# Eight of the 22 weight slots of the first feed-forward's up product computed as 2x2 block products

## The chip, the core and the metric

The kernel runs on one core of one Trainium2 chip. The metric is device time in microseconds (us) of one execution; of the kernel before, three runs are shown. A profiled execution gives the rows quoted below; its times count from its first instruction. Engines: PE is TensorE, DVE is VectorE, ACT is ScalarE, POOL is GpSimd, SP is SyncE, which here only issues weight transfers.

## What is computed

Two transformer blocks over 512 tokens of width 1024 in float32. The part that matters is the first block's feed-forward, whose up product `h @ w_up` has 5632 columns, followed by a causal convolution of width 3 along the tokens, a gelu on one half and a product with the other half:

```python
D_MODEL = 1024; SEQ = 512; D_FF = 2816; CONV_WIDTH = 3
h = _rmsnorm(x, g_pre_ffn[i])
u = _causal_dwconv(h @ w_up[i], w_conv[i], b_conv[i])
a, v = u[..., :D_FF], u[..., D_FF:]
x = x + _rmsnorm((jax.nn.gelu(a) * v) @ w_down[i], g_post_ffn[i])
```

The second block has two further feed-forwards (`up0`/`down0`, `up1`/`down1`) of width 4096 with a squared relu.

## The kernel before, in words

**Split products.** Every float32 product is made of three fp32r matmuls: both operands are split into a high part (ACT copies to fp32r) and a low part (DVE subtracts the high part from the original), and high x high, high x low and low x high are summed in PSUM. So each weight block costs ACT one "high" copy (`L1074`) and DVE one "low" subtraction (`L1745`) before PE may use it; semaphores `w_hi` and `w_lo` count them.

**Weight ring.** SP loads weights in slots of 1 MB (two transfers of 512 KB) into `raw`, which has two places. Slot n may be loaded when both ends of slot n-2 have been split. The split halves go to `WHL`, a ring of six half places of 128x512. A unit of 128x1024 takes two half places, a block of 128x512 takes one. `upto(w)` says which units may be split once unit w has been used by PE.

**The up stage.** `w_up` has 22 slots (j = 0 to 21). Slot j holds 128 columns of the a half and the 128 columns of the v half that belong to them: two units, s = 0 and 1. For each unit PE makes one group: 8 steps of k x 3 matmuls with 512 token columns, into one of banks 0 to 3 (`feature_product`, lines 2609 to 2611). The first four groups are made in two token halves by `norm_halves`. When a group is done, ACT scales it by the last tap into `cv` (`L1488`), DVE adds the other two taps, reading the bank again (`L2213`, two instructions), ACT takes the gelu of the a half (`L1496`) and DVE multiplies (`L2224`) into `uT`. Each engine works through a written-out order, so an instruction that waits holds up all behind it on its engine. ACT and DVE split a weight unit after each unit of the convolution.

**The block product of the second block's feed-forwards.** In `up0` and `up1` the last 12 slots are computed otherwise. The slot's 1024x256 weights are read as 2x2 blocks A11, A12, A21, A22 (512x128 each), the activations as B11, B12, B21, B22 (512x256 each), and seven products replace eight. POOL makes four sums of weight blocks per slot (S1, S2, S4, S3, lines 864 to 869), DVE makes four sums of activation blocks once per feed-forward, PE makes seven products of 12 matmuls with 256 columns (lines 3321 to 3323), ACT copies the first result (`st_m1`), and DVE adds the results with seven 128x256 additions (`L2410`). S1 and S2 lie in `GB`, S4 in `PB`, S3 over A11's place in `raw`.

Of the kernel before, what the change touches and what calls it, by code (L numbers as in the profile page):

```python
# [26 lines left out]
F32 = mybir.dt.float32  # L27
# [53 lines left out]
NSUM = 7  # L81

# [29 lines left out]
def weight_slots(t):  # L112
# [86 lines left out]
    for name in ("kq0",) + DENSE_KV:  # L199
# [3 lines left out]
        else:  # L203
# [12 lines left out]
          ("merge", 16, "act"), ("br", 16, "vec"), ("up", 2 * NFF, "conv"),  # L216
# [3 lines left out]
          ("dv1", 4, "vec"), ("kq3", 4, "act"), ("up1", NCL, "act")]  # L220

# [62 lines left out]
def strassen_slot(name, i):  # L284

    return name in UPS and 2 * i >= NCL
# [6 lines left out]
def program(nc, t, out):  # L293
    with ExitStack() as ctx:
# [68 lines left out]
        cv = PB[:, 0:3072].rearrange("p (b a t) -> p b a t", b=2, a=3)  # L363
# [166 lines left out]
        lhs_sum, rhs_sum, rhs_hi, rhs_lo = (sem(s) for s in ("lhs_sum", "rhs_sum", "rhs_hi", "rhs_lo"))  # L530
        st_full, st_keep, st_sum, sq_ready = (sem(s) for s in (
# [25 lines left out]
        for n, (name, i, _) in enumerate(slots):  # L557
            if strassen_slot(name, i):
                for j, part in enumerate(LHS):
                    unit_at[name, part, i - NCL // 2] = len(units)  # L560
# [36 lines left out]
        for n, (name, i, _) in enumerate(slots):  # L597
            g0 = GT[name][0] if name in GT else None
            if strassen_slot(name, i):
                for j in range(len(LHS)):  # L600
                    unit_free.append((st_full, len(LHS) * (NPAIR * int(name[2:]) + i - NCL // 2) + j + 1))
                slot_free.append((w_lo, len(unit_free)))
            elif name not in WHOLE:
                for j in range(2):
# [189 lines left out]
        def _(pool):  # L794
# [58 lines left out]
            def block_sums(l, gain):  # L853

                n, name = 4 + 2 * l, UPS[l]

                def lhs_sums(q):

                    i = slot_at[name, NCL // 2 + q]
                    at = len(SUMS) * (NPAIR * l + q)  # L860
# [11 lines left out]
                for q in range(NPAIR):  # L872
                    lhs_sums(q)
                if gain is not None:
                    pool.wait_ge(w_lo, unit_at[name, "S1", NPAIR - 1] + 1)
                    pool.dma_start(GB[:, :], gain.to_broadcast([P, D])).then_inc(gain_in, 16)

            def resid(r):
# [33 lines left out]
                if r in (3, 5):  # L912
                    block_sums((r - 3) // 2, nxt[r + 1])
# [92 lines left out]
            pool.wait_ge(x_ready, 4)  # L1006
            pool.dma_start(ptok, t["p"][0, 0].rearrange("(t p) c -> p t c", p=P)).then_inc(p_in, 16)
# [59 lines left out]
        def _(act):  # L1067
# [10 lines left out]
            def split(w):  # L1078

                while done[0] <= min(w, n_units - 1):  # L1080
# [5 lines left out]
                    elif strassen_slot(*slots[units[u][0]][:2]) and LHS[units[u][1]][0] == "S":  # L1086
                        name, i = slots[units[u][0]][:2]
                        q = NPAIR * int(name[2:]) + i - NCL // 2
# [388 lines left out]

            for j in range(NFF):
                if j == 10:
                    for k in range(2):  # L1480
                        act.wait_ge(pt_in_psum, k + 1)
                        copy(pTh[:, k, :], bank[4 + k][:, :]).then_inc(pt_hi, 1)
                if j >= 2:
                    act.wait_ge(u_ready, j - 1)
                for s in range(2):
                    f = s * NFF + j
                    wait_group("up", 2 * j + s)
                    a.activation(cv[:, j % 2, s, :], bank[(GT["up"][0] + 2 * j + s) % 4][:, :], ACT.Identity,  # L1488
                                 bias=cols[:, C_BCONV + f:C_BCONV + f + 1],
                                 scale=tapcol(2, f)).then_inc(conv_act, 1)  # L1490
                    if f < 2 * NFF - 1:
                        split(unit_at["up", 2 * j + s] + HL)
                    if j == NFF - 1 and s == 0:
                        rows_begin(uT, "down", lambda k: (u_ready, k + 1))
                act.wait_ge(conv_vec, 2 * j + 1)
# [59 lines left out]
            def mlp(name, l):  # L1555
# [24 lines left out]
                for c in range(NCL):  # L1580
                    plain(c)
                    if c in (1, 2, 3, 4):
                        rhs_high(c - 1)
                    if c >= 2:
                        split(upto(unit_at[name, c]))
                for q in range(NPAIR):
                    n = NPAIR * l + q
                    split(upto(unit_at[name, "A11", q]))
                    act.wait_ge(st_full, len(LHS) * n + 2)
                    if n:  # L1590
                        act.wait_ge(st_sum, NSUM * (n - 1) + 2)
                    copy(st_m1, st_bank(q, 0)).then_inc(st_keep, 1)
# [127 lines left out]
        def _(vec):  # L1720
# [477 lines left out]

            for j in range(NFF):
                if j == 10:  # L2200
                    for k in range(2):
                        vec.wait_ge(pt_hi, k + 1)
                        v.tensor_tensor(pTl[:, k, :], bank[4 + k][:, :], pTh[:, k, :].bitcast(F32),
                                        ALU.subtract).then_inc(pt_lo, 1)
                for s in range(2):
# [3 lines left out]
                    b = wait_group("up", 2 * j + s)  # L2209
                    vec.wait_ge(conv_act, 2 * j + s + 1)  # L2210
                    y = cv[:, j % 2, s, :]
                    for tap, sh in ((1, 1), (0, 2)):
# [5 lines left out]
                        else:  # L2218
                            ins.then_inc(conv_vec, 1)
                    if f < 2 * NFF - 1:  # L2220
                        split(unit_at["up", 2 * j + s] + HL)
                vec.wait_ge(conv_vec, 2 * j + 2)
# [1323 lines left out]
```

## Time and profile before

| What | Value |
|---|---|
| Median of 3 runs | 2040.4 us (2039.64 to 2042.12) |
| Profiled execution, its own time | 2039.82 us |
| Its span, first to last instruction | 2038.1 us |
| PE busy | 2017.6 us, 99% of the span |
| DVE, ACT, POOL busy | 1227.8, 928.0, 411.6 us |
| Up stage on PE, groups 5 to 44 | 427.3 to 645.8 us |
| Granted TensorE clock | 0.999 of full speed |

The time of the execution is 1.7 us above its span. A row of the timeline gives start, duration, engine, line, operation, what it writes and reads, and how many in a row; durations of neighbours overlap by about 0.1 us, so the distance between two starts, called the pitch below, says what an instruction costs its engine.

### The profile page before, as it was taken

Reading aid. Unit: us, or ns where it says so; the run is one execution under the profiler, and the core shown is the slowest. Engines: PE = TensorE matmul, PEld = TensorE weight load, DVE = VectorE, ACT = ScalarE, POOL = GpSimd, SP = SyncE. Lnnn points to the kernel's source line nnn. Section 1 sums busy time; section 2 is a strip of 40 time slices with the busy share of each in tenths; the row PEclk is TensorE's granted clock in tenths of the full one; section 3 lists DMA queues with packets and bytes.
Section 4 is the critical chain, followed back from the end, with each engine's and each line's share of the span. In section 5 each row is a group of like instructions: output and inputs, shape, how many; then the busy total and the mean of one; then the engine's idle time right before and its main releaser. Section 6 shows DMA issues by size and latency. Waiting matters only on the chain.

```text
span 2038.1 us, 31753 instructions
## 1 busy us (share of the span) xinstructions
PE 2017.6 (99%) x12798; PEld 1695.7 (83%) x12798; DVE 1227.8 (60%) x2042; ACT 928.0 (46%) x1708; POOL 411.6 (20%) x402
## 2 busy tenths in 40 slices
PE   8999999999999999999999999999999999999998
PEld 7987567888888888878888999888877779999887
DVE  4744766565555344676676899433655558897334
ACT  4345664443333334523335566322545556665322
POOL 7500000000000000223331365000533112562000
PEclk9999999999999999999999999999999999999999
DMA  7336412333333222222213233332332232233222
GB/s 170 102 96 91 58 42 93 94 104 103 95 92 104 103 104 93 79 83 80 84 43 104 80 100 109 118 104 96 121 94 83 73 101 66 84 104 135 104 85 81
DMA packets 167535, 191.18 MB, mean 94 GB/s; under 512 B 18818, under 2 KB 137133, under 8 KB 167389
## 3 DMA queue, kind: packets, MB, share of 16 engines
q1 hardware_dynamic: 163469, 175.25, 27.3%
q0 software_dynamic: 3904, 13.90, 3.7%
q8 instruction: 101, 1.65, 0.3%
q14 instruction: 45, 0.37, 0.1%
q10 hardware_dynamic: 16, 0.00, 0.0%
HBM read 181.79 MB, written 7.34 MB: 93 GB/s over the span
## 4 chain that ended last, share of the span: by engine, by line
PE 96%; DVE 2%; ACT 1%; issue 0%; POOL 0%; DMA 0%; POOLq 0%; DVEq 0%; ACTq 0%
PE bank L2710 27%; PE bank L2609 9%; PE bank L2610 8%; PE bank L2611 8%; PE bank L3323 4%; PE bank L3322 4%; PE bank L3321 4%; PE bank L2648 2%; PE bank L2650 2%; PE bank L2649 2%; PE bank L3224 2%; PE bank L2881 1%; PE bank L3226 1%; PE bank L3225 1%; PE bank L3245 1%; PE bank L3247 1%
## 5 line engine op out<-in xcount | busy, mean ns | idle before, releaser
L1745 DVE TENSOR_TENSOR WHL<-raw,WHL 128x1024 fp32r<-128x1024 f32 (+2 forms) x357 | 458.7, 1292 | 441.9 <-ACT WHL L1074 441.6
L1074 ACT ACTIVATE WHL<-raw 128x1024 fp32r<-128x1024 f32 (+2 forms) x357 | 334.1, 939 | 511.3 <-PE bank L2710 325.3
L2710 PE MATMUL bank<-WHL,HXh 128*128 128x512 f32 x1344 | 362.3, 390 | 0.0
L2609 PE MATMUL bank<-HXh,WHL 128*128 128x512 f32 x752 | 298.3, 397 | 0.0
L2710 PEld LDWEIGHTS bank<-WHL,HXh 128*128 128x128 f32 x1344 | 251.3, 188 | 52.8 <-issue 1.2
L2611 PE MATMUL bank<-HXh,WHL 128*128 128x512 f32 x752 | 293.2, 390 | 0.0
L2610 PE MATMUL bank<-HXl,WHL 128*128 128x512 f32 x576 | 224.3, 389 | 0.0
L2710 PE MATMUL bank<-WHL,HXl 128*128 128x512 f32 x672 | 208.4, 389 | 0.0
L2609 PEld LDWEIGHTS bank<-HXh,WHL 128*128 128x128 f32 x752 | 141.1, 188 | 33.3 <-issue 3.7
L2611 PEld LDWEIGHTS bank<-HXh,WHL 128*128 128x128 f32 x752 | 141.1, 188 | 30.3
L888 POOL TENSOR_SCALAR small<-small 128x1 f32<-128x1 f32 x24 | 7.8, 324 | 761.0 <-ACT PB L1162 760.9
L2710 PEld LDWEIGHTS bank<-WHL,HXl 128*128 128x128 f32 x672 | 126.1, 188 | 26.2
L2213 DVE SCALAR_TENSOR_TENSOR PB<-bank,cols,PB 128x511 f32<-128x511 f32 x88 | 66.0, 750 | 101.6 <-ACT PB L1488 100.0
L2610 PEld LDWEIGHTS bank<-HXl,WHL 128*128 128x128 f32 x576 | 108.3, 188 | 21.1
L1488 ACT ACTIVATE PB<-bank,cols 128x512 f32<-128x512 f32 x44 | 34.4, 781 | 141.8 <-PE bank L2611 136.0
L830 POOL TENSOR_TENSOR raw<-raw,cols 128x1024 f32<-128x1024 f32 x24 | 46.0, 1932 | 221.7 <-DMA raw<-in_b_w_q_dram 211.2
L3323 PE MATMUL bank<-HXh,WHL 128*128 128x256 f32 x288 | 81.5, 283 | 0.0
L3322 PE MATMUL bank<-HXl,WHL 128*128 128x256 f32 x288 | 81.5, 283 | 0.0
L3321 PE MATMUL bank<-HXh,WHL 128*128 128x256 f32 x288 | 81.5, 283 | 0.0
L2610 PE MATMUL bank<-HX2l,WHL 128*128 128x512 f32 x176 | 68.6, 390 | 0.0
L1025 POOL TENSOR_TENSOR PB<-BIG,PB 128x512 f32<-128x512 f32 x24 | 39.6, 1650 | 142.3 <-PE bank L3188 101.3
L864 POOL TENSOR_TENSOR GB<-raw 128x512 f32<-128x512 f32 x24 | 38.8, 1616 | 138.4 <-DVE WHL L1745 91.3
(380 smaller groups left out, 4440.8 us busy)
## 6 DMA issues: line engine op xcount, KB each, us to landing
raw<-in_mlp_w_up_dram SPq DMA_DIRECT2D x64, 512.0 KB, 4.7
raw<-in_mlp_w_down_dram SPq DMA_DIRECT2D x64, 512.0 KB, 4.1
raw<-in_w_up_dram SPq DMA_DIRECT2D x44, 512.0 KB, 5.1
raw<-in_a_w_in_dram SPq DMA_DIRECT2D x32, 512.0 KB, 4.6
raw<-in_w_in_dram SPq DMA_DIRECT2D x22, 512.0 KB, 4.8
raw<-in_w_down_dram SPq DMA_DIRECT2D x22, 512.0 KB, 3.7
raw<-in_w_kv_dram SPq DMA_DIRECT2D x16, 512.0 KB, 4.5
rel_dram<-GB POOLq DMA_DIRECT2D x1, 5120.0 KB, 54.5
```

Source lines behind the costliest of these rows:

```text
L830: g.tensor_tensor(w, w, cols[:, c:c + nk].unsqueeze(2).to_broadcast([P, nk, D // nk]), ALU.mult).then_inc(w_scaled, 1)
L1074: return a.activation(dst, src, ACT.Copy, **k)
L1745: v.tensor_tensor(dst(1), src, dst(0).bitcast(F32), ALU.subtract).then_inc(w_lo, 1)
L2213: ins = v.scalar_tensor_tensor(out=y[:, sh:T], in0=b[:, 0:T - sh], scalar=tapcol(tap, f), in1=y[:, sh:T], op0=ALU.mult, op1=ALU.add)
L2609: m.matmul(b[:, :], w[0][:, k, :], x[0][:, k, :], start=(k == 0), stop=False)
L2610: m.matmul(b[:, :], w[0][:, k, :], x[1][:, k, :], start=False, stop=False)
L2611: return m.matmul(b[:, :], w[1][:, k, :], x[0][:, k, :], start=False, stop=(k == KD - 1))
L2648: m.matmul(b[:, sl], wh[:, k, :], HXh[:, k, sl], start=(k == 0), stop=False)
L2710: ins = m.matmul(ybank(tt, h, 1 if name == "down" else 0)[:, :], x, w[:, h * HALF:(h + 1) * HALF], start=(k == 0 and i == 0), stop=(k == n ...
L3321: m.matmul(dst, wh[:, k, :], x[0][:, k, :], start=(k == 0), stop=False)
L3322: m.matmul(dst, wh[:, k, :], x[1][:, k, :], start=False, stop=False)
L3323: ins = m.matmul(dst, wl[:, k, :], x[0][:, k, :], start=False, stop=(k == KD // 2 - 1))
```

## The change

Slots j = 6, 8, 10, ..., 20 of the up stage (`UPJ`) become block products; the odd slots and the first six stay as they were. For such a slot:

- PE makes 84 matmuls with 256 columns instead of 48 with 512, into banks 4 to 7. Before each block slot but the first it waits until all seven additions of the last one are done.
- ACT and DVE split seven blocks of 128x512 instead of two units of 128x1024.
- POOL makes four 128x512 sums; ACT copies one 128x256 result; DVE makes seven additions. The sums land in `uT`, and the convolution then reads `uT` (SBUF) instead of the bank.
- DVE makes the activation sums in slots 0 to 3 (nine 128x1024 instructions), ACT their high parts in slots 1 to 4, DVE their low parts in slots 4 and 5.
- A slot of blocks takes seven of the ring's half places; the eighth is skipped and counted as used by the last block.

`cv` moves from `PB` to `BIG`, S4 to `BIG`, the transposes of the other input from slot 10 to slot 9, its load ahead of POOL's block sums, and the load of `g_post_ffn` behind them. The code for `up0` and `up1` becomes shared functions with the same order of work.

```diff
+PTURN = 9
+UPJ = (6, 8, 10, 12, 14, 16, 18, 20)
...
-    return name in UPS and 2 * i >= NCL
+    return name in UPS and 2 * i >= NCL or name == "up" and i in UPJ
...
-                ring_before[w] = latest.get(ring_place[w] + n - 1)
+                ring_before[w] = max((latest[ring_place[w] + h] for h in range(n) if ring_place[w] + h in latest),
+                                     default=None)
                 for h in range(n):
                     latest[ring_place[w] + h] = w
                 half_place += n
+                if slots[units[w][0]][0] == "up" and n == 1 and units[w][1] == len(LHS) - 1:
+                    latest[half_place % (2 * HL)] = w
+                    half_place += 1
...
+            def pair_begin(name, q):
+
+                n = PAIR0[name] + q
+                split(upto(unit_at[name, "A11", q]))
+                act.wait_ge(st_full, len(LHS) * n + 2)
+                if n:
+                    act.wait_ge(st_sum, NSUM * (n - 1) + 2)
+                copy(partial(name)[0], st_bank(name, q, 0)).then_inc(st_keep, 1)
+
             for j in range(NFF):
...
                 if j >= 2:
                     act.wait_ge(u_ready, j - 1)
+                if j in (1, 2, 3, 4):
+                    rhs_high(0, j - 1)
+                if j in UPJ:
+                    q = UPJ.index(j)
+                    pair_begin("up", q)
+                    for part in LHS[1:]:
+                        split(upto(unit_at["up", part, q]))
...
+            def pair_sums(name, q, row1, row2, early=None, late=None):
...
+                vec.wait_ge(st_full, at + 2)
+                vec.wait_ge(st_keep, n + 1)
+                add(c11, m1, 1)
+                split(upto(unit_at[name, "A11", q]))
+                split(upto(unit_at[name, "A12", q]))
+                vec.wait_ge(st_full, at + 4)
+                add(u2, m1, 3)
+                split(upto(unit_at[name, "S4", q]))
+                split(upto(unit_at[name, "S2", q]))
...
             for j in range(NFF):
...
+                if j in (4, 5):
+                    for i in (0, 1) if j == 4 else (2, 3):
+                        rhs_low(0, i)
+                if j in UPJ:
+                    q = UPJ.index(j)
+                    pair_sums("up", q, uT[:, j, :], uT[:, j + 1, :])
                 for s in range(2):
                     f = s * NFF + j
...
-                    b = wait_group("up", 2 * j + s)
+                    b = uT[:, j + s, :] if j in UPJ else wait_group("up", conv_tile(j, s))
...
+                    if j in UPJ:
+                        if s:
+                            split(upto(unit_at["up", "A22", q]))
+                    elif f < 2 * NFF - 1:
+                        split(upto(unit_at["up", 2 * j + s]))
...
+                if j < 4:
+                    rhs_block(0, j, 1)
...
+            for j in range(2, NFF):
+                if j in UPJ:
+                    q = UPJ.index(j)
+                    if q:
+                        pe.wait_ge(st_sum, NSUM * q)
+                    if j > PTURN:
+                        pe.wait_ge(pt_lo, 2)
+                    block_pair("up", q)
+                    continue
```

**How it stands on DVE, slots 12 and 13.** Before, two slots are twice this piece (two taps from a bank, one weight unit, again, the product; line numbers are of before):

```order
L2213 SCALAR_TENSOR_TENSOR PB<-bank0,cols,PB 128x511 [waits conv_act,ps_full]
L2213 SCALAR_TENSOR_TENSOR PB<-bank0,cols,PB 128x510 [waits vec_chain]
L1745 TENSOR_TENSOR WHL<-raw,WHL 128x1024 [waits w_hi]
L2213 SCALAR_TENSOR_TENSOR PB<-bank1,cols,PB 128x511 [waits conv_act,ps_full]
L2213 SCALAR_TENSOR_TENSOR PB<-bank1,cols,PB 128x510 [waits vec_chain]
L1745 TENSOR_TENSOR WHL<-raw,WHL 128x1024 [waits w_hi]
L2224 TENSOR_TENSOR BIG<-PB 128x512 [waits gelu_ready,conv_vec]
```

In the changed kernel the block slot begins with the additions (`L2286`); the last block, A22, is split behind the first of them, and then come the taps from SBUF, the next block slot's first two blocks, and the product (line numbers are of the changed kernel, `L1791` is the split):

```order
L2286 TENSOR_TENSOR BIG<-PB,bank4 128x256 [waits st_keep,st_full]
L1791 TENSOR_TENSOR WHL<-raw,WHL 128x512 [waits w_hi]
L2286 TENSOR_TENSOR BIG<-PB,bank5 128x256 [waits st_full]
L1791 TENSOR_TENSOR WHL<-raw,WHL 128x1024 [waits w_hi]
L2286 TENSOR_TENSOR BIG<-BIG,bank6 128x256 [waits st_sum,st_full]
...
L1791 TENSOR_TENSOR WHL<-raw,WHL 128x1024 [waits w_hi]
L2330 SCALAR_TENSOR_TENSOR BIG<-BIG,cols 128x511 [waits conv_act]
L2330 SCALAR_TENSOR_TENSOR BIG<-BIG,cols 128x510 [waits vec_chain]
L2330 SCALAR_TENSOR_TENSOR BIG<-BIG,cols 128x511 [waits conv_act]
L2330 SCALAR_TENSOR_TENSOR BIG<-BIG,cols 128x510 [waits vec_chain]
L1791 TENSOR_TENSOR WHL<-raw,WHL 128x512 [waits w_hi] x2
L2349 TENSOR_TENSOR BIG<-BIG 128x512 [waits gelu_ready,st_conv]
```

What moved: the next block slot's A11 and A12 now stand behind four tap instructions whose two large operands both lie in SBUF.

**How it stands on ACT, slot 1.** Before, the gelu of slot 0 (`L1496`) is followed at once by the first convolution instruction of slot 1; after (`L1550` is the gelu, `L1102` the copies) one copy stands between them that waits for the activation sum `rhs_sum`. Before:

```order
L1496 ACTIVATE PB<-PB 128x512 [waits conv_vec]
L1488 ACTIVATE PB<-bank2,cols 128x512 [waits ps_full]
```

and after:

```order
L1550 ACTIVATE BIG<-BIG 128x512 [waits conv_vec]
L1102 ACTIVATE HX2l<-PB 128x1024 [waits rhs_sum]
```

What moved: the convolution of slot 1 and the weight copy behind it now come after DVE's first activation sum, which on DVE is three 128x1024 instructions behind the product of slot 0.

## Rows read from the trace of the kernel before

**Rows 1.** The page, busy time and share of the span of each engine.
```profile
PE 2017.6 (99%) x12798; PEld 1695.7 (83%) x12798; DVE 1227.8 (60%) x2042; ACT 928.0 (46%) x1708; POOL 411.6 (20%) x402
```

**Rows 2.** Waits, 420 to 650 us: who waited for whom, total, times, longest.
```profile
ACT PB L1488 <- PE bank L2611: 136.0, 40, 3.7
DVE PB L2213 <- ACT PB L1488: 100.0, 44, 2.7
```

**Rows 3.** Line 2611 in 424 to 646 us: count, durations in ns, first and last start.
```profile
L2611 PE MATMUL bank<-HXh,WHL x320: 389/389/393, 427.7 to 645.6; 128*128 128x512 f32 x160
```

**Rows 4.** Timeline of PE: transposes in the up stage; first block matmul, end of `up0`.
```profile
514.35 1.03 PE L3090 MATMUL bank<-ident,BIG 128*128 128x128 f32 x8
515.14 0.48 PE L2609 MATMUL bank<-HXh,WHL 128*128 128x512 f32 x1
...
1152.68 0.28 PE L3321 MATMUL bank<-HXh,WHL 128*128 128x256 f32 x1
...
1273.63 1.55 PE L2710 MATMUL bank<-WHL,HX2l 128*128 128x512 f32 x6
```

**Rows 5.** Timeline of ACT and DVE in the up stage, one unit.
```profile
503.66 0.78 ACT L1488 ACTIVATE PB<-bank,cols 128x512 f32<-128x512 f32 x1 [3.65 <-PE bank L2611]
504.34 1.05 ACT L1074 ACTIVATE WHL<-raw 128x1024 fp32r<-128x1024 f32 x1
...
504.55 1.53 DVE L2213 SCALAR_TENSOR_TENSOR PB<-bank,cols,PB 128x511 f32<-128x511 f32 x2 [2.71 <-ACT PB L1488]
506.00 1.22 DVE L1745 TENSOR_TENSOR WHL<-raw,WHL 128x1024 fp32r<-128x1024 f32 x1
507.13 0.69 DVE L2224 TENSOR_TENSOR BIG<-PB 128x512 f32<-128x512 f32 x1
```

**Rows 6.** Timeline of DVE and POOL in `up0`, one block slot.
```profile
1176.82 3.16 DVE L1745 TENSOR_TENSOR WHL<-raw,WHL 128x512 fp32r<-128x512 f32 x2
1179.91 0.41 DVE L2410 TENSOR_TENSOR PB<-PB,bank 128x256 f32<-128x256 f32 x1
1180.24 1.45 DVE L1745 TENSOR_TENSOR WHL<-raw,WHL 128x512 fp32r<-128x512 f32 x1
...
1183.64 1.07 DVE L2410 TENSOR_TENSOR BIG<-PB,bank 128x256 f32<-128x256 f32 x3
1184.64 0.68 DVE L1745 TENSOR_TENSOR WHL<-GB,WHL 128x512 fp32r<-128x512 f32 x1
1185.24 0.41 DVE L2410 TENSOR_TENSOR BIG<-BIG,bank 128x256 f32<-128x256 f32 x1
...
1177.81 1.63 POOL L866 TENSOR_TENSOR GB<-GB,raw 128x512 f32<-128x512 f32 x1
1179.51 1.62 POOL L868 TENSOR_TENSOR PB<-raw,GB 128x512 f32<-128x512 f32 x1
```

**Rows 7.** Timeline of POOL and DVE at the first block sums of `up0`.
```profile
1139.67 1.29 POOL L866 TENSOR_TENSOR GB<-GB,raw 128x512 f32<-128x512 f32 x1
1141.04 2.16 POOL L868 TENSOR_TENSOR PB<-raw,GB 128x512 f32<-128x512 f32 x1
...
1139.76 2.29 DVE L1745 TENSOR_TENSOR WHL<-raw,WHL 128x1024 fp32r<-128x1024 f32 x1 [1.32 <-ACT WHL L1074]
```

**Rows 8.** Slot loads: SP's issues of one slot; the page's time to landing.
```profile
447.46 0.99 SPq L778 DMA_DIRECT2D raw<-in_w_up_dram  x2
...
raw<-in_w_up_dram SPq DMA_DIRECT2D x44, 512.0 KB, 5.1
```

**Rows 9.** Timeline of ACT in `up0`, two high parts of blocks.
```profile
1171.42 1.14 ACT L1074 ACTIVATE WHL<-GB 128x512 fp32r<-128x512 f32 x2
```

**Rows 10.** Timeline of DVE, first activation sum of `up0`: three instructions from 1121.21.
```profile
1121.21 1.22 DVE L2383 TENSOR_TENSOR PB<-HXl 128x1024 f32<-128x1024 f32 x1
...
1124.85 1.22 DVE L2376 TENSOR_TENSOR PB<-HXh,PB 128x1024 f32<-128x1024 f32 x1
```

**Rows 11.** Timeline of DVE, product of slot 0 in the up stage.
```profile
424.54 0.69 DVE L2224 TENSOR_TENSOR BIG<-PB 128x512 f32<-128x512 f32 x1 [0.41 <-ACT PB L1496]
```

More of the change, by code:

```diff
@@ L2197, in _ @@
             border(0)
-            for j in range(NFF):
[L2200 to L2204, printed above, removed]
+            (b11, b11l), (b12, b12l), (b21, b21l), (b22, b22l) = (
+                [x.bitcast(F32) for x in rhs(part)] for part in ("B11", "B12", "B21", "B22"))
@@ L3085, in _, with block @@
             norm_halves(1)
[L3086 to L3092 removed]
+            def block(name, q, part, x, i):
+                w = unit_at[name, part, q]
+                pe.wait_ge(w_lo, w + 1)
+                wh, wl = (split_buf(w, j).rearrange("p (k c) -> p k c", k=KD // 2) for j in range(2))
+                dst = st_bank(name, q, i)
+                for k in range(KD // 2):
+                    m.matmul(dst, wh[:, k, :], x[0][:, k, :], start=(k == 0), stop=False)
+                    m.matmul(dst, wh[:, k, :], x[1][:, k, :], start=False, stop=False)
+                    ins = m.matmul(dst, wl[:, k, :], x[0][:, k, :], start=False, stop=(k == KD // 2 - 1))
+                ins.then_inc(st_full, 1)
@@ new lines, in block_pair @@
+            def block_pair(name, q):
+                o = 4 * SETS.index(name)
+                block(name, q, "A11", rhs("B11"), 0)
+                block(name, q, "A12", rhs("B21"), 1)
+                block(name, q, "S4", rhs("B22"), 2)
+                if q == 0:
+                    pe.wait_ge(rhs_lo, o + 2)
+                block(name, q, "S2", rhs_sums(1), 3)
+                block(name, q, "S1", rhs_sums(0), 4)
+                if q == 0:
+                    pe.wait_ge(rhs_lo, o + 3)
+                block(name, q, "S3", rhs_sums(2), 5)
+                if q == 0:
+                    pe.wait_ge(rhs_lo, o + 4)
+                block(name, q, "A22", rhs_sums(3), 6)
@@ new lines, in _ @@
+            for j in range(2, NFF):
+                if j in UPJ:
+                    q = UPJ.index(j)
[5 more added lines that the diff above has]
+                    continue
+                for s in range(2):
+                    if j == PTURN and s:
+                        pe.wait_ge(p_in, 16)
+                        pe.wait_ge(st_sum, NSUM * sum(1 for i in UPJ if i < j))
+                        for k in range(2):
+                            for tt in range(TT):
+                                ins = m.transpose(bank[4 + k][:, tt * P:(tt + 1) * P],
+                                                  ptok[:, tt, k * P:(k + 1) * P], ident[:, :])
+                            ins.then_inc(pt_in_psum, 1)
+                    w = [y.rearrange("p (k c) -> p k c", k=KD) for y in unit("up", 2 * j + s)]
+                    b = group("up", conv_tile(j, s))
+                    for k in range(KD):
+                        ins = feature_product(b, w, (HXh, HXl), k)
+                    ins.then_inc(ps_full, 1)
@@ L3308, in _, with block_pairs @@
                     out_product(k, (tt,))
[L3310 to L3324 removed]
+            def block_pairs(name):
                 for q in range(NPAIR):
```

267 lines of the change are left out of this document (128 added, 139 removed).

## The prediction

> **What bounds the kernel now.** I read the page first: PE is busy 99% of the span, DVE 60%, ACT 46% [rows 1]. Then the waits of the up stage, to see who sets its pace: ACT waits 136.0 us there for PE, once in each of 40 groups, DVE waits 100.0 us for ACT, and PE's feature products wait for nobody [rows 2]. So the up stage lasts as long as PE's matmuls, and each microsecond of PE work removed is gained, as long as DVE, ACT, POOL and the slot loads still keep ahead.
>
> **PE, removed.** One matmul with 512 columns costs the distance to the next. Line 2611 is every third of 960 matmuls: from the first to the last of its 320 starts there are 217.9 us and 957 steps [rows 3], with the transposes between (514.35 to 515.14, 0.8 us [rows 4]): 217.1/957 = 0.227 us. A plain slot has 48: 10.89 us. A matmul with 256 columns: the 12 block slots of `up0` take 1152.68 to 1273.63 for 1008 matmuls, 0.120 us each, with no stall [rows 4]. A block slot has 84: 10.08 us. Eight slots save 8 x 0.81 = **6.5 us**, 0.32%. That is all the change can give. About 0.2% (4.1 us) is what a measurement of this kernel can tell from no change.
>
> **DVE, added.** Pitches: two tap instructions from a bank 1.45 us, a 128x1024 low part 1.13 [rows 5]; a 128x256 addition 0.33, a 128x512 low part 0.60 [rows 6], the product likewise 0.60. Taps that read only SBUF stand in no row: not below 0.60 (the 128x512 instruction of two SBUF operands [rows 6]), not above 0.75 (the bank taps with their semaphore); I take 0.70, nearest the bank taps, since the same chain wait stays. A plain slot costs 2 x 1.45 + 2 x 1.13 + 0.60 = 5.8 us; a block slot 7 x 0.33 + 7 x 0.60 + 4 x 0.70 + 0.60 = 9.9. Together 15.7 of the 20.97 us that PE now has for two slots. That alone would fit.
>
> **What POOL does to DVE.** While POOL makes block sums, DVE's instructions on two SBUF operands come out longer: two 128x512 low parts take 3.09 us from start to start instead of 1.20, 0.94 us more each; a third takes 1.45 instead of 0.68. The addition between them reads a bank and keeps its 0.41 [rows 6]. With a larger neighbour: a low part issued at 1139.76, just behind POOL's 1139.67, ends at 1142.05, so with its own 1.22 it began at 1140.83, 1.16 after POOL; and POOL's next, issued at 1141.04, takes 2.16 because it now waits for DVE [rows 7]. So the two take turns, and POOL holds DVE for 0.94 to 1.16 us a time; I take 1.05. Four sums a slot give DVE up to 4.2 us more: 19.9 of 20.97. And the change puts the taps of block slots (BIG,cols and BIG) among the instructions that are held, which the bank taps are not.
>
> The Trainium skill (SBUF — State Buffer, "Who interferes with whom" and the reading of its diagram) states this as a lock: a VectorE instruction with two SBUF inputs and a GpSimd instruction that reads SBUF exclude each other for the whole instruction. If the whole recorded 1.62 us of a POOL sum were the hold, DVE would need 15.7 + 6.5 = 22.2 of 20.97 us and each pair of slots would be 1.2 us late; the rows of this case give 1.05, since 1.62 includes POOL's own wait for DVE.
>
> **The loop that decides.** Average load is not enough, because there is a ring of waits from one block slot's A22 to the next, with no PE in it:
> 1. A22's low part done, so SP loads the next block slot: the second issue about 0.5 us after the first, landed 5.1 later [rows 8], semaphore 0.1: 5.7.
> 2. ACT's high parts of A11 and A12 come ahead of its convolution instruction: 1.05 (1.14 less the overlap) [rows 9], then 0.89 from ACT's start to DVE's [rows 5]: 1.9.
> 3. Four taps, 2.8. POOL starts its sums with the same landing, so its second is running when the taps begin: held 0.4 + 1.05 + 1.05 = 2.5. Together 5.3.
> 4. Low parts A11, A12 (1.2), product (0.6), next plain slot's taps (1.45), S4 and S2 (1.2), taps (1.45), S1 and S3 (1.2), product (0.6), first addition (0.33), A22 (0.7): 8.7.
>
> Sum 21.6 us against 20.97 on PE: **0.65 us late per round**. Being late shows first at PE's A11 and S4: A11's low part is ready 5.7 + 1.9 + 5.3 + 0.6 + 0.2 = 13.7 after the last A22, so A22 may be 7.2 us into its slot at most; S4 follows A11 by 3.3 us where PE allows 2.9, so 6.9. At the first block slot the two late activation parts (2 x 1.13), the taps, four blocks, the product, an addition and A22 put A22 at about 6.5. That leaves 0.4 of slack; seven rounds cost 7 x 0.65 - 0.4 = 4.2 us.
>
> **The start.** DVE ends slot 0's product at 425.2 [rows 11]. The first activation sum is three instructions, 3.64 us to the next start [rows 10]: 428.8. Only then ACT makes its high part (0.95), the convolution of slot 1 (0.68) and the high part of the sixth unit (0.95): 431.4. DVE does its taps from 430.7 to 432.1, the low part to 433.3. PE's fifth group began at 427.3, two matmuls ahead of the first start in [rows 3], and ends 24 x 0.227 = 5.4 later, at 432.7: 0.6 us of stall. At slots 4 and 5, four low parts of 1.13 meet POOL's first sums, which hold DVE up to four times; the unit needed there would be ready about 0.3 late (between 0 and 2). Start: **1.0 us**.
>
> At no cost: ACT, whose added 2.1 us per two slots (7 x 0.53 + 0.3 less 2 x 0.95) lie in its 136 us of waiting [rows 2]; the moved transposes (same number); the moved `g_post_ffn` load, needed only behind `down`; PE's wait for all additions, which has a plain slot of 10.9 us between, and would cost only if DVE were that late.
>
> **Sum:** -6.5 + 1.0 + 4.2 = -1.3 us on the profiled execution's 2039.82: 2038.5. The median of the runs shown lies 0.6 above that execution: **2039.1**.
>
> **Rivals.**
> - *Full gain.* The loop is 0.65 too long by terms of which I am not sure: with 0.63 for an SBUF tap (-0.3), holds of 0.95 (-0.3) and a landing 0.2 earlier it is below 20.97 and only the start remains: -6.5 + 0.6 to 1.0, so 2034.5 to 2034.9. For it: DVE's sum of 19.9 fits. Against: the order of waits above. Up to a loop of 21.3 it is still faster by over 4.1.
> - *Slower.* The same loop, longer: holds of 1.16 (+0.3), taps of 0.75 (+0.2), a landing 0.3 later and another hold on the low parts A11, A12 (+1.05 every round if POOL's fourth sum reaches them). From 22.3 us on it decides: 7 x 1.4 - 0.4 + 1.0 - 6.5 = +3.9; with the whole lot 23.2, +10: 2050.
> - *A hold of 1.62 us each time,* POOL's recorded duration: the holds in step 3 grow by 3 x 0.57, loop 23.3, +12: 2052. The turns in [rows 6, 7] speak against it; I give it 0.02, inside the slower rival. (It is what the rule of the Trainium skill, SBUF — State Buffer, gives if the recorded span is taken for the instruction's own.)
> - *The start alone costs more:* 2 to 3 us, if the high part that ACT makes ahead of each slot's convolution delays slots 2 to 4 as well. There each sum is two instructions and PE allows more than 1 us. Then 2041, within the same case.
>
> **How the numbers follow.** Loop between 21.0 and 22.2, result -4.1 to +4: 0.58. Full or nearly full gain: 0.28. Slower by over 0.2%: 0.14. Faster, same and slower are these three. The range goes to 2034.5, the full gain, and to 2044, as the slow rival beyond it has about 1 in 10.
>
> **What the changed profile would show.** The block line in the up stage at 0.120 us a matmul, a block slot 10.1 us where nothing is late. PE waiting about 0.6 us in the sixth group and 0.3 to 1 us at A11 or S4 of the later block slots, ended by DVE's low part. DVE taps in block slots of 1.7 to 1.8 us where they meet POOL, 0.7 where not. DVE over 90% busy from slot 6 on. Period of two slots 21.3 to 21.8 us. The prediction is wrong if that period is 20.97 (loop short enough), or over 22.3; also if PE waits for the additions instead of the low parts, which I did not price.

## The result and the profile after

| | Before | Changed |
|---|---|---|
| Median | 2040.12 us (2039.64 to 2042.12, 6 runs) | 2048.34 us (2046.93 to 2049.06, 6 runs) |
| Span of the profiled execution | 2038.1 us | 2046.4 us |
| PE, first matmul of `down` | 645.79 us | 653.46 us |

The ratio is 1.0038, with a 95% interval from 1.0028 to 1.0049: the changed kernel is 8.2 us slower. The prediction was 2039.1 us with a range to 2044.0, so it was wrong, and on the wrong side of the range. Of the 8.3 us by which the span grew, 7.7 us have arisen by the end of the up stage; 0.6 us come behind it.

The page of the changed kernel, busy time by engine, and the share of the engines in the chain that ended last. In the page of before the chain was PE for 96%:

```profile
PE 2016.9 (99%) x13086; PEld 1706.6 (83%) x13086; DVE 1295.7 (63%) x2151; ACT 949.8 (46%) x1760; POOL 461.2 (23%) x434
...
PE 86%; DVE 7%; DMA 3%; ACT 2%; issue 2%; POOL 0%; SPq 0%; POOLq 0%; DVEq 0%; ACTq 0%
```

PE has hardly less busy time than in [rows 1], although 6.5 us of matmuls were to go; and 12% of the chain now run over DVE, DMAs and ACT, where it was 3% before. Both ask for PE's own rows. The timeline of PE in the changed kernel, those rows at which it had waited (`L2682` to `L2684` are the plain matmuls, `L3168` to `L3170` those of the blocks, `L2785` is `down`):

```profile
433.27 0.50 PE L2682 MATMUL bank<-HXh,WHL 128*128 128x512 f32 x1 [0.45 <-DVE WHL L1791]
...
514.43 0.39 PE L2684 MATMUL bank<-HXh,WHL 128*128 128x512 f32 x1
520.67 0.55 PE L3168 MATMUL bank<-HXh,WHL 128*128 128x256 f32 x1 [5.85 <-DVE pb_rest L2345]
...
586.61 0.36 PE L3168 MATMUL bank<-HXh,WHL 128*128 128x256 f32 x1 [0.25 <-DVE WHL L1791]
...
653.46 2.77 PE L2785 MATMUL bank<-WHL,HX2h 128*128 128x512 f32 x11 [1.79 <-DVE HX2h L1800]
```

The large one stands ahead of slot 10: 514.43 to 520.67 where 0.23 is the pitch, 6.0 us lost. Its releaser is not a weight block but `pb_rest`, the low parts of the transposes of the other input (`pe.wait_ge(pt_lo, 2)` for j > PTURN in the diff): the transposes lie in banks 4 and 5, which the block slot writes over, so they must have been split first. What follows the pause is in the windows of PE, DVE, ACT and POOL there; PEclk is the granted clock as a share of 2.4 GHz:

```profile
core 0: us, PE busy (x) PEld busy (x) DVE busy (x) ACT busy (x) POOL busy (x), PEclk, DMA share, GB/s
510.00:515.00 5.00, 4.82 (x22) 3.66 (x20) 4.93 (x5) 2.58 (x6) 3.51 (x3) 1.00 0.00 1
515.00:520.00 5.00, 0.00 (x0) 0.00 (x0) 4.96 (x9) 3.12 (x6) 0.00 (x0) 0.94 0.00 0
520.00:525.00 5.00, 4.33 (x20) 4.36 (x21) 3.78 (x6) 0.63 (x1) 0.00 (x0) 0.50 0.00 0
525.00:530.00 5.00, 5.00 (x40) 5.00 (x39) 1.44 (x3) 1.21 (x2) 0.00 (x0) 0.88 0.19 54
```

After the pause PE runs at the lower of its two levels, 1.2 GHz. Of the rows of the timeline of PE, two before and two behind the return of the clock show it in the pitch, 0.21 and 0.12 us:

```profile
525.50 0.41 PE L3169 MATMUL bank<-HXl,WHL 128*128 128x256 f32 x1
525.72 0.41 PE L3170 MATMUL bank<-HXh,WHL 128*128 128x256 f32 x1
...
526.41 0.28 PE L3168 MATMUL bank<-HXh,WHL 128*128 128x256 f32 x1
526.53 0.28 PE L3169 MATMUL bank<-HXl,WHL 128*128 128x256 f32 x1
```

Some 26 matmuls cost 0.21 instead of 0.12 us; block slot 10 lasts 12.57 us (520.67 to 533.24) instead of 10.07. That is a part of why PE's busy time hardly shrank, and not the larger one. From 427.2 us to `down` PE is busy for 218.6 us before and 217.3 here; e1_turn3 below, whose clock stays up, still has 216.5, and e6_all, which has no stalls, 212.1. A short stall shows only in part as idle time: the row behind it is longer (0.36 us at 586.61, where the rows beside it have 0.28) and overlaps the wait. The Trainium skill (TensorE: Matmul & The Clock Gate, "What's actually happening") says that the throttled state is the default and work releases the clock; the rows agree, 0.94 in the window without a matmul and 0.50 right behind it.

Where the 7.7 us come from, by the starts of PE's slots (plain slots otherwise 10.90, block slots 10.08):

| Term | Predicted | Measured |
|---|---|---|
| Matmuls removed | -6.5 | -6.5 |
| Start, up to slot 6 (first block matmul at 471.7) | +1.0 | +1.0 |
| Pause ahead of slot 10 | 0 | +6.1 |
| Lower clock in slot 10 | 0 | +2.5 |
| Stalls in all other slots from 6 to 20 | +4.2 | +2.5 |
| Slot 21, ahead of `down` | 0 | +2.0 |
| Sum | -1.3 | +7.6 |

The 6.1 us of the pause are slot 9's 17.81 us less the 10.90 of a plain slot and 0.8 for the transposes; the gap between the two rows gives 6.0.

Now the loop. ACT, POOL and DVE around the landing of slot 16, and PE at S4 of that slot, as the timelines have them (`L1102` high parts, `L1537` convolution, `L2330` taps, `L891` to `L896` POOL's sums, `L895` being S4):

```profile
577.08 0.99 SPq L804 DMA_DIRECT2D raw<-in_w_up_dram  x2
...
578.42 1.16 ACT L1102 ACTIVATE WHL<-raw 128x512 fp32r<-128x512 f32 x2 [3.24 <-DMA raw<-in_w_up_dram]
578.46 1.30 POOL L891 TENSOR_TENSOR GB<-raw 128x512 f32<-128x512 f32 x1 [15.71 <-DMA raw<-in_w_up_dram]
...
579.48 1.51 ACT L1537 ACTIVATE BIG<-BIG,cols 128x512 f32<-128x512 f32 x2
579.84 1.30 POOL L893 TENSOR_TENSOR GB<-GB,raw 128x512 f32<-128x512 f32 x1
...
580.31 5.55 DVE L2330 SCALAR_TENSOR_TENSOR BIG<-BIG,cols 128x511 f32<-128x511 f32 x4 [3.26 <-ACT BIG L1537]
...
581.22 1.61 POOL L895 TENSOR_TENSOR BIG<-raw,GB 128x512 f32<-128x512 f32 x1
...
582.80 1.73 POOL L896 TENSOR_TENSOR raw<-raw 128x512 f32<-128x512 f32 x1
...
585.78 1.29 DVE L1791 TENSOR_TENSOR WHL<-raw,WHL 128x512 fp32r<-128x512 f32 x2
...
589.03 0.68 DVE L1791 TENSOR_TENSOR WHL<-BIG,WHL 128x512 fp32r<-128x512 f32 x1
...
589.77 0.39 PE L3168 MATMUL bank<-HXh,WHL 128*128 128x256 f32 x1
```

One landing starts three engines. ACT makes two high parts first, from 578.42 to 579.48, and only then the convolution for which DVE waits, idle for 3.26 us; by then POOL is in its second sum, and DVE's four taps take 5.47 us (580.31 to 585.78). PE is 0.2 us late at S4 as well (589.77, 0.34 behind its last matmul of A12 where 0.12 is the pitch); POOL had made S4 at 582.83, and what came last was DVE's low part, at 589.71. The groups by form, 475 to 650 us (count, busy us, mean ns of one), show the two kinds of taps side by side:

```profile
L2330 DVE SCALAR_TENSOR_TENSOR BIG<-BIG,cols 128x511 f32<-128x511 f32 x16 | 23.5, 1471 | 24.3 <-ACT BIG L1537 24.3
L2330 DVE SCALAR_TENSOR_TENSOR BIG<-BIG,cols 128x510 f32<-128x510 f32 x16 | 18.4, 1149 | 0.6
L2330 DVE SCALAR_TENSOR_TENSOR BIG<-bank,cols,BIG 128x510 f32<-128x510 f32 x15 | 11.2, 749 | 0.5
L2330 DVE SCALAR_TENSOR_TENSOR BIG<-bank,cols,BIG 128x511 f32<-128x511 f32 x15 | 11.2, 744 | 0.0
```

With both large operands in SBUF a tap takes 1.47 or 1.15 us, from a bank 0.75.

### The profile page after: what moved, and what is told of

Its sections match the earlier page's. It is cut to its first block, busy times and chain, and to the rows that moved or that the text cites. A ratio compares the mean times of both kernels' runs of the same rounds, so it can differ in the third digit from the quotient of the medians.

```text
span 2046.4 us, 32576 instructions
## 1 busy us (share of the span) xinstructions
PE 2016.9 (99%) x13086; PEld 1706.6 (83%) x13086; DVE 1295.7 (63%) x2151; ACT 949.8 (46%) x1760; POOL 461.2 (23%) x434
## 4 chain that ended last, share of the span: by engine, by line
PE 86%; DVE 7%; DMA 3%; ACT 2%; issue 2%; POOL 0%; SPq 0%; POOLq 0%; DVEq 0%; ACTq 0%
PE bank L2785 27%; PE bank L2682 5%; PE bank L2684 5%; PE bank L2683 5%; PE bank L3168 4%; PE bank L3170 4%; PE bank L3169 4%; DVE BIG L2330 2%; DMA raw<-in_w_up_dram 2%; PE bank L2721 2%; PE bank L2723 2%; PE bank L2722 2%; DVE WHL L1791 2%; PE bank L3344 1%; PE bank L2956 1%
## 5 line engine op out<-in xcount | busy, mean ns | idle before, releaser
L1791 DVE TENSOR_TENSOR WHL<-raw,WHL 128x1024 fp32r<-128x1024 f32 (+2 forms) x373 | 461.4, 1245 | 442.6 <-ACT WHL L1102 442.3
L1102 ACT ACTIVATE WHL<-raw 128x1024 fp32r<-128x1024 f32 (+2 forms) x373 | 336.5, 907 | 577.5 <-PE bank L2785 328.3
L2785 PE MATMUL bank<-WHL,HXh 128*128 128x512 f32 x1344 | 362.3, 390 | 0.0
L2785 PEld LDWEIGHTS bank<-WHL,HXh 128*128 128x128 f32 x1344 | 251.4, 188 | 52.8 <-issue 1.2
L2682 PE MATMUL bank<-HXh,WHL 128*128 128x512 f32 x624 | 248.9, 399 | 0.5 <-DVE WHL L1791 0.5
L2684 PE MATMUL bank<-HXh,WHL 128*128 128x512 f32 x624 | 243.4, 390 | 0.0
L2785 PE MATMUL bank<-WHL,HXl 128*128 128x512 f32 x672 | 208.4, 389 | 0.0
L2683 PE MATMUL bank<-HXl,WHL 128*128 128x512 f32 x448 | 174.7, 390 | 0.0
L2785 PEld LDWEIGHTS bank<-WHL,HXl 128*128 128x128 f32 x672 | 126.1, 188 | 26.2
L2682 PEld LDWEIGHTS bank<-HXh,WHL 128*128 128x128 f32 x624 | 117.2, 188 | 29.2 <-issue 4.0
L2684 PEld LDWEIGHTS bank<-HXh,WHL 128*128 128x128 f32 x624 | 117.2, 188 | 25.3
L891 POOL TENSOR_TENSOR GB<-raw 128x512 f32<-128x512 f32 x32 | 50.0, 1562 | 304.0 <-DMA raw<-in_w_up_dram 165.7
L3168 PE MATMUL bank<-HXh,WHL 128*128 128x256 f32 x384 | 110.6, 288 | 6.8 <-DVE pb_rest L2345 5.9
L3169 PE MATMUL bank<-HXl,WHL 128*128 128x256 f32 x384 | 109.7, 286 | 0.0
L3170 PE MATMUL bank<-HXh,WHL 128*128 128x256 f32 x384 | 109.7, 286 | 0.0
L2683 PEld LDWEIGHTS bank<-HXl,WHL 128*128 128x128 f32 x448 | 84.3, 188 | 15.9
L3168 PEld LDWEIGHTS bank<-HXh,WHL 128*128 128x128 f32 x384 | 74.8, 195 | 9.2 <-issue 8.2
L3169 PEld LDWEIGHTS bank<-HXl,WHL 128*128 128x128 f32 x384 | 74.9, 195 | 0.2
L3170 PEld LDWEIGHTS bank<-HXh,WHL 128*128 128x128 f32 x384 | 74.8, 195 | 0.0
L3168 PE MATMUL bank<-HX2l,WHL 128*128 128x256 f32 x256 | 72.4, 283 | 0.0
```

The source lines that it names most:

```text
L891: g.tensor_tensor(lhs(i, "S1"), lhs(i, "A21"), lhs(i, "A22"), ALU.add).then_inc(lhs_sum, 1)
L1102: return a.activation(dst, src, ACT.Copy, **k)
L1791: v.tensor_tensor(dst(1), src, dst(0).bitcast(F32), ALU.subtract).then_inc(w_lo, 1)
L2682: m.matmul(b[:, :], w[0][:, k, :], x[0][:, k, :], start=(k == 0), stop=False)
L2683: m.matmul(b[:, :], w[0][:, k, :], x[1][:, k, :], start=False, stop=False)
L2684: return m.matmul(b[:, :], w[1][:, k, :], x[0][:, k, :], start=False, stop=(k == KD - 1))
```

## The experiments

The theory after reading the trace: POOL's hold makes DVE late (the loop); at slot 10 the same lateness meets the wait for the transposes' low parts, and the clock drops behind it. The rivals: that the transposes' new place alone does the damage (then the kernel with them elsewhere shows the full gain); that the SBUF taps are slow by themselves. "D" is how the first matmul of `down` stands to 645.79 of before.

| Kernel | Median (range), us | Ratio to before, 95% | D, us |
|---|---|---|---|
| e1_turn3 | 2045.05 (2044.22 to 2046.04) | 1.0024 [1.0015, 1.0033] | +4.5 |
| e2_turn3_tiny | 2034.98 (2034.17 to 2035.43) | 0.9975 [0.9965, 0.9985] | -5.6 |
| e10_tiny9 | 2034.81 (2034.57 to 2035.27) | 0.9974 [0.9964, 0.9984] | -5.5 |
| e3_actfirst | 2038.97 (2037.12 to 2039.31) | 0.9993 [0.9984, 1.0002] | -0.9 |
| e4_four | 2037.74 (2037.58 to 2038.90) | 0.9989 [0.9980, 0.9998] | -2.3 |
| e5_both | 2035.91 (2035.68 to 2036.53) | 0.9980 [0.9971, 0.9989] | -4.2 |
| e7_late | 2036.93 (2035.56 to 2038.21) | 0.9985 [0.9976, 0.9994] | -2.2 |
| e9_ptfirst | 2035.52 (2034.87 to 2036.24) | 0.9977 [0.9969, 0.9986] | -4.7 |
| e6_all | 2033.81 (2033.71 to 2033.99) | 0.9970 [0.9958, 0.9981] | -6.5 |

The kernel before had a median of 2039.8 to 2040.0 us beside them.

**The transposes moved to slot 3.**

```diff
-PTURN = 9
+PTURN = 3
```

> The changed kernel with one number changed: the eight transposes of the other input stand in slot 3 instead of slot 9, long before the first block slot, so no block slot waits for their low parts on DVE. Theory A (two separate losses: 6.1 us of waiting for these low parts plus 2.4 us of matmuls at the lower TensorE clock behind it; and a loop of waits DVE - slot load - ACT - taps - DVE of 21.8 us against 20.97 on PE): the 8.5 us go, but the 6.1 us pause had also given the loop slack, and without it seven rounds late by 0.8 us come back, with 2 us at the start of down: -6.5 + 1.0 + 5.2 + 2 = +1.7 us against the kernel before, about 2042. Theory B (the transposes alone throw DVE late; the loop is a consequence): nearly the full gain, -5.5 us, about 2034.6.

Measured: 2045.05. The pause and the clock's drop are gone, but only 3.3 us came back. The period from one block slot to the next is now 21.5, 22.1, 22.3, 22.0, 21.7, 21.9 and 21.7 us, 6.4 us in all over 7 x 20.98, and slot 21 lasts 12.71 us. So the loop is too long from the first round on. In the changed kernel it cost only 2.5 us because the pause and the slow slot behind it, 8.6 us together, had given DVE time to catch up: the first whole round in its wake is at 20.98, the next three at 21.5, 21.8 and 21.7. The rival of the place alone is out. PE's waiting row ahead of slot 10 is now of the size and kind predicted for the loop:

```profile
517.49 0.36 PE L3168 MATMUL bank<-HXh,WHL 128*128 128x256 f32 x1 [0.59 <-DVE WHL L1791]
```

The start is 2.4 us late here: DVE makes the transposes' low parts at 453.42 (1.2 us), and the activation sums' low parts behind them come under POOL's first sums for longer (4.57 instead of 3.46 us for two). The 2042 expected was missed by 3 us: the start cost 2.4 and not 1.0, the rounds 6.4 and not 5.2.

**The same, with POOL's sums of this feed-forward cut to 8 of 512 elements.** The weight sums are thereby left out of the computation; DVE, ACT and PE do all their instructions.

```diff
+def part_of_block(i, part):
+    return lhs(i, part)[:, 0:1, 0:8] if name == "up" else lhs(i, part)
...
-g.tensor_tensor(lhs(i, "S1"), lhs(i, "A21"), lhs(i, "A22"), ALU.add).then_inc(lhs_sum, 1)
+g.tensor_tensor(part_of_block(i, "S1"), part_of_block(i, "A21"), part_of_block(i, "A22"), ALU.add).then_inc(lhs_sum, 1)
```

and so for S2, S4 and S3.

> As the run with the transposes in slot 3, and POOL's four block sums of each block slot of the first feed-forward are cut to 8 elements per partition (that part of the weight sums is left out; the order, the waits and all other work stay). Theory A with POOL's hold as its decisive term: the taps take 2.8 to 3.0 us instead of 5.5 and the loop falls to about 19.2 us, below 20.97: no stall at block slots, only the start's 1.0 us, -5.5 us, about 2034.6. If DVE is late by its own added work and not by POOL, the time is that of the run with full sums.

Measured: 2034.98. Every block slot lasts 10.08, every plain slot 10.90 us, with no stall after the start. The groups by form of DVE, 475 to 640 us:

```profile
L2334 DVE SCALAR_TENSOR_TENSOR BIG<-BIG,cols 128x510 f32<-128x510 f32 x16 | 12.0, 751 | 0.6
L2334 DVE SCALAR_TENSOR_TENSOR BIG<-BIG,cols 128x511 f32<-128x511 f32 x16 | 12.0, 748 | 11.1 <-ACT BIG L1541 11.1
```

The SBUF taps take the 0.75 us of a bank tap. They are not slow; POOL held them. This kernel takes both POOL's hold and the time of the sums away and cannot by itself tell one from the other; but where PE waited for S4 in the rows above, POOL had made it 6.9 us before DVE's low part was done.

**The same cut (the weight sums left out), with the transposes in slot 9** as in the changed kernel.

```diff
-PTURN = 3
+PTURN = 9
```

> The changed kernel with the transposes left in slot 9, and POOL's block sums of the first feed-forward cut to 8 elements on one of the four sub-blocks (so the weight sums are left out of the computation). The slots before showed a pause of 5.85 us ahead of the block slot after the transposes. If that pause is only DVE's being late, and DVE is late only because POOL holds it, the pause goes together with the loop: block slot 10 at 10.1 us, clock 1.0, and a time within 1 us of the same cut with the transposes in slot 3 (2035.0), so 2034.5 to 2035.5. If the place of the transposes costs a wait of its own (their low parts stand behind taps and a weight split on DVE, whoever held it), a pause of 2 to 6 us stays in slot 9 and the time is 2037 to 2043.

Measured: 2034.81. The timelines of DVE and PE:

```profile
505.55 2.98 DVE L2334 SCALAR_TENSOR_TENSOR BIG<-BIG,cols 128x511 f32<-128x511 f32 x4 [1.35 <-ACT BIG L1541]
...
512.90 1.28 DVE L2349 TENSOR_TENSOR pb_rest<-bank,pb_rest 128x512 fp32r<-128x512 f32 x2
...
514.01 0.39 PE L2688 MATMUL bank<-HXh,WHL 128*128 128x512 f32 x1
514.28 0.36 PE L3172 MATMUL bank<-HXh,WHL 128*128 128x256 f32 x1
```

against these of the changed kernel:

```profile
500.31 5.38 SPq L804 DMA_DIRECT2D raw<-in_w_up_dram  x4
...
507.47 1.15 ACT L1102 ACTIVATE WHL<-raw 128x512 fp32r<-128x512 f32 x2 [4.73 <-DMA raw<-in_w_up_dram]
...
509.37 5.55 DVE L2330 SCALAR_TENSOR_TENSOR BIG<-BIG,cols 128x511 f32<-128x511 f32 x4 [4.75 <-ACT BIG L1537]
514.83 1.29 DVE L1791 TENSOR_TENSOR WHL<-raw,WHL 128x512 fp32r<-128x512 f32 x2
...
519.29 1.28 DVE L2345 TENSOR_TENSOR pb_rest<-bank,pb_rest 128x512 fp32r<-128x512 f32 x2
```

The pause goes with the hold: one root for both losses. With DVE free the low parts end at about 514.2, and PE goes on at 514.28, 0.05 us late: the wait has no slack at all, and whatever DVE is late there, PE is late in full. In the changed kernel the taps start 3.8 us later (509.37 against 505.55) and take 2.6 us more; the low parts start 6.4 us later. Of the 3.8 us, 2.6 are the slot load's issue (500.31 against 497.74, because DVE's low part of A22 was late by as much after the held taps of the round before), and 1.3 its landing (7.2 us from issue to ACT's start against 5.9).

**ACT's order.** In a block slot ACT makes its two convolution instructions, and only then the high parts of A11 and A12 that wait for the slot load.

```diff
-                    for part in LHS[1:]:
+                    for part in LHS[1:-1]:
                         split(upto(unit_at["up", part, q]))
...
+                if j in UPJ:
+                    split(upto(unit_at["up", "A22", q]))
                 act.wait_ge(*((st_conv, 2 * q + 1) if j in UPJ else (conv_vec, conv_tile(j) + 1)))
```

> The changed kernel with one thing moved on ACT: in a block slot its two convolution instructions stand ahead of the high parts of the next block slot's A11 and A12, which wait for the slot's load. The transposes stay in slot 9. Theory A: DVE's taps begin about 3 us earlier, before POOL's sums, and leave the loop, which falls to about 18 to 19 us; the waiting for the transposes' low parts shrinks from 6.1 to 1 to 3 us, and the clock stays up if the pause is short; the 2 us at the start of down go. -6.5 + 1.0 + 1 to 3 = -4.5 to -2.5 us, about 2036.6. Theory B: the wait in slot 10 stays as it is, 2045 or above.

Measured: 2038.97. The work is the same, and from slot 12 on every round is at 20.98 us. The timeline of ACT and DVE in slot 14:

```profile
571.29 1.52 ACT L1537 ACTIVATE BIG<-BIG,cols 128x512 f32<-128x512 f32 x2 [0.33 <-DVE BIG L2288]
573.28 1.15 ACT L1102 ACTIVATE WHL<-raw 128x512 fp32r<-128x512 f32 x2 [0.48 <-DMA raw<-in_w_up_dram]
...
572.75 5.85 DVE L2332 SCALAR_TENSOR_TENSOR BIG<-BIG,cols 128x511 f32<-128x511 f32 x4
```

The convolution no longer waits for the landing, so the taps start before it and are off the loop; they are held just as much (1.44 and 1.13 us each). But the pause ahead of slot 10 is still 2.8 us, and the matmuls behind it run at the lower clock. This kernel missed the 2036.6 us expected of it by 2.4 us for that reason: taking the convolution off the loop does not shorten the queue ahead of the transposes' low parts enough. The slow matmuls seem not to come in every execution: of its eleven, eight have a span of 2037.0 to 2037.2 us, as the profiled one, and three have 2035.3, 2035.3 and 2036.0. The difference is about the 1.5 us of the clock, but these three left no trace, so this is not shown.

**Both edits,** the transposes in slot 3 and ACT's order.

```diff
-PTURN = 9
+PTURN = 3
...
-                    for part in LHS[1:]:
+                    for part in LHS[1:-1]:
...
```

> Transposes in slot 3 and ACT's two convolution instructions ahead of the next A11 and A12, together. If the two losses are separate and the loop is broken by the second move: -6.5 + 2.4 (the start as the profile of the run with the transposes in slot 3 shows it) + 0 in the block slots = -4 us, 2036. If moving the transposes early costs rounds of the loop whatever stands on ACT: near 2042 or above.

Measured: 2035.91. All seven rounds are 20.98 us; what is left is the start, 2.4 us.

**Four block slots,** three plain ones between them, transposes in slot 9.

```diff
-UPJ = (6, 8, 10, 12, 14, 16, 18, 20)
+UPJ = (6, 10, 14, 18)
```

> Only slots 6, 10, 14 and 18 as block products, transposes in slot 9 as in the change. PE saves 3.2 us. Theory A: two plain slots more lie between block slots, so the loop has 42.7 us and is never late, DVE is on time in slot 9 and the transposes' low parts cost PE at most 1 us: -3.2 + 1.0 + 0 to 1 = -2 us, 2038. Theory B (the transposes in slot 9 cost a wait whatever the load): +6 us, 2046.

Measured: 2037.74. No block slot waits, slot 10 starts without a pause although the transposes stand in slot 9, and D is -2.3: 4 x 0.81 saved, 1.0 of start lost. Half the slots give more than all eight do, for then a round has 42.7 us.

**ACT's order, and the high parts of the activation sums behind the gelu.**

```diff
                 if j >= 2:
                     act.wait_ge(u_ready, j - 1)
-                if j in (1, 2, 3, 4):
-                    rhs_high(0, j - 1)
...
                 a.activation(cv[:, j % 2, 2, :], cv[:, j % 2, 0, :], ACT.Gelu_apprx_tanh).then_inc(gelu_ready, 1)
+                if j in (1, 2, 3, 4):
+                    rhs_high(0, j - 1)
```

> The changed kernel with ACT's convolution ahead of the next A11 and A12 and with the late high parts; transposes in slot 9. Against the run with the first move alone (2038.97) 0.6 to 1.0 us less: 2038.2. The wait for the transposes' low parts (2.8 us) and the lower clock behind it (1.5 us) stay.

Measured: 2036.93. The first block slot starts at 470.5 us instead of 471.8, with no stall in the sixth group: the start's 1.0 us was ACT's wait for the first activation sum, and the order alone removes it. The pause ahead of slot 10 is the same as in e3_actfirst. The profiled execution, 2038.02, is what was expected (2038.2); the median lies 1.3 below that, since six of the eleven spans are 2033.5 to 2035.1 us and five 2035.9 to 2036.3, the profiled one among these.

**The same, with the transposes' high and low parts ahead of the weight parts in slot 9,** on ACT and on DVE (the cut shows DVE).

```diff
+                    if j == PTURN and s == 0:
+                        for k in range(2):
+                            vec.wait_ge(pt_hi, k + 1)
+                            v.tensor_tensor(pTl[:, k, :], bank[4 + k][:, :], pTh[:, k, :].bitcast(F32),
+                                            ALU.subtract).then_inc(pt_lo, 1)
                     if j in UPJ:
                         if s:
                             split(upto(unit_at["up", "A22", q]))
...
```

> As the run before, and in slot 9 the transposes' high parts (ACT) and low parts (DVE) stand ahead of the weight splits. DVE reaches the low parts 1.2 us earlier: the pause before the block slot 10 falls from 2.8 to about 1.6 us. If the clock fell because of the length of the pause, the shorter one keeps it: 1.2 + 1.5 = 2.7 us less, 2035.5; if it falls after any pause: 1.2 us less, 2037.

Measured: 2035.52. Windows of e7_late and then of this kernel, 515 to 525 us:

```profile
515.00:520.00 5.00, 3.87 (x23) 3.90 (x24) 4.24 (x7) 1.52 (x3) 0.00 (x0) 0.75 0.00 0
520.00:525.00 5.00, 5.00 (x41) 5.00 (x40) 1.66 (x4) 1.45 (x2) 0.00 (x0) 0.91 0.31 91
```

```profile
515.00:520.00 5.00, 4.88 (x41) 4.91 (x42) 4.96 (x10) 2.07 (x5) 0.00 (x0) 1.00 0.00 0
520.00:525.00 5.00, 5.00 (x44) 5.00 (x43) 3.03 (x6) 1.98 (x2) 0.00 (x0) 1.00 0.72 193
```

The pause is 1.2 us shorter (1.6 us) and the clock stays at 2.4 GHz, so slot 10 lasts 10.14 instead of 11.62 us: D is 2.5 us better. The medians differ by 1.4 us only, as the runs of e7_late spread from 2035.56 to 2038.21 and its profiled execution, with 2038.02, is one of its longest; e9_ptfirst spreads from 2034.87 to 2036.24.

**All three:** the edits of e7_late with the transposes in slot 3.

```diff
-PTURN = 9
+PTURN = 3
```

> As the run before, and ACT makes the high parts of the activation sums behind the gelu of slots 1 to 4 instead of ahead of their convolution. If the 0.6 to 1.0 us at PE's sixth group come from ACT waiting there for DVE's first sum, they go: 0.6 to 1.0 us below the run with both moves, about 2035.2. If they come from DVE's added work itself: the same time as that run.

Measured: 2033.81, the fastest, 0.9970 of before with the interval from 0.9958 to 0.9981. That is 1.4 us below the 2035.2 expected: ACT's order took away all 2.4 us of e5_both's start, and not only 0.6 to 1.0. PE's first matmul of `down`, with no wait ahead of it, and none since 427 us:

```profile
639.25 7.95 PE L2787 MATMUL bank<-WHL,HX2h 128*128 128x512 f32 x34
```

645.79 less 639.25 is 6.54 us: all that the matmuls removed can give. It has all eight block slots, POOL's sums and holds included.

## Why the prediction was wrong

**The step that failed** is the list "at no cost": "the moved transposes (same number)". Their number is the same, but their place has a wait behind it that before did not bind: PE may not start slot 10 until DVE has made their low parts, and on DVE these stand behind four held taps, two blocks, a product, two bank taps and two more blocks. I named that queue in no step, though the diff has the wait and the instructions' order shows it. Even with DVE free they come 0.05 us late (e10_tiny9). It cost 6.1 us, and the pause then cost 2.5 us more in the clock, a term that the sum did not have. e1_turn3 bears that out in part only: moving the transposes alone gave back 3.3 us, since the loop then came up in full.

**The slower rival** was built on the loop alone, from 22.3 us on. It came true by a different place: a loop of about the predicted length, and a wait that it feeds. I asked for every block at which being late shows, A11 and S4, and not for waits of other kinds in the same stretch.

**The loop** was right in mechanism and size per round. Four taps were put at 5.3 us and took 5.47; the loop at 21.6 us, and the last rounds of the changed kernel take 21.8, those of e1_turn3 21.9 on average. Step by step, from the end of A22's low part at 572.71 to the next at 594.50: 5.7 us to ACT's start (put at 5.7), 1.9 to the taps (1.9), 5.5 (5.3) and 8.7 (8.7). PE waits where the prediction said, at A11 (0.4 us) and S4 (0.2 to 0.3). So 0.65 us a round was a little low (0.9 in e1_turn3); the sum of 4.2 was 6.4 in e1_turn3, and 2.5 in the changed kernel, where the pause reset it. That the stalls of the changed kernel came out below 4.2 is the pause's doing and no merit of the sum. The cure shows the same: it is the order of waits and not DVE's load, for e3_actfirst leaves the load and loses the stalls.

**The hold** of 1.05 us a time was right within what the rows can tell: four taps cost 5.47 - 4 x 0.75 = 2.5 us more, as the step had it. The Trainium skill (SBUF — State Buffer, "Who interferes with whom") says that a VectorE instruction with two SBUF inputs and a GpSimd instruction that reads SBUF exclude each other; e2_turn3_tiny agrees, 0.75 us a tap without POOL's sums, 1.47 and 1.15 beside them. The rival of 1.62 us a hold is out: it asked for a loop of 23.3 us.

**The start** was right: 1.0 us, 0.6 of it at 433.27, ended by DVE's low part, and e7_late shows its cause.

**The sums of the rivals** do not all come out of their own terms. The slower rival's whole lot adds up to 21.6 + 1.85 = 23.45 us and +11.5, not 23.2 and +10; the hold of 1.62 gives 7 x 2.34 - 5.9 = +10.5, not +12; and "faster by over 4.1" holds up to a loop of 21.2, not 21.3. The forecast uses none of them.

**The full gain** of 6.5 us was right as a bound; e6_all has it. **DVE over 90% busy** was wrong: it is busy for 74.7 of the 88 us from 565 to 653, 85%. A loop of waits can set the pace with its engines idle in turn.

**Slot 21** was not priced. DVE comes late to `down`'s first low parts, which PE awaits (1.8 us in the chain of its row at 653.46); it is there in e1_turn3 (12.71 us) and gone in every kernel without stalls, so it is the loop's lateness again, at the one place where no later slot hides it.

Open: the 0.6 us of span behind the up stage; the same difference is 0.2 us in e6_all and none in e5_both, but 0.5 in e2_turn3_tiny, which has no stalls, so it does not follow them. Not tried: the wait for the low parts with the transposes in banks of their own.

## What to carry to other kernels

A loop of waits that holds no work of the bounding engine is summed up against that engine's period, and the cure is to take one member out of it by order: here the convolution went ahead of the copies that wait for a load, and the rounds fell from 21.9 to 20.98 us. When work is moved, look for every wait that names its semaphore and write down what stands ahead of the signalling instruction on its engine at the new place; "same number" says nothing of that. And price one more thing for a pause on PE: what the clock does behind it.

## What was unexpected in the hardware

- The granted clock fell to 0.50 in the pause of 6.0 us, and some 26 matmuls took 0.21 instead of 0.12 us (2.5 us in all). After pauses of 2.8 us (e3_actfirst, e7_late) block slot 10 lasted 11.62 us, 1.5 too long, at 0.74 and 0.75 in the window from 515 to 520. In e3_actfirst the first matmul behind the pause was slow already; in e7_late PE had gone on for 1.4 us at a pitch of 0.12 before it fell to 0.21, at 517.52. After 1.6 us (e9_ptfirst) the clock stayed at 1.00.
- By the chain that ended last, the landing of a slot took 5.2 to 5.3 us in five rounds of the up stage and 6.7 in two, the one ahead of the pause (500.73) and the one behind it (528.12). Four loads within 5.4 us are not the reason: they were issued so at 500.31, but also at 572.74, where the landing took 5.2. What made the two longer stays open.
